# Linear stages of a two-block transformer: the three products of each row tile in a row, in place of three passes

## The chip, the cores and the metric

One core of a Trainium2 chip runs the whole program. The metric is device time in microseconds (us), as the median of several executions. Engines: PE is TensorE's matmul row and PEld its weight loads, DVE is VectorE, ACT is ScalarE, POOL is GpSimd, SP is SyncE, which issues the DMAs.

## The reference, cut to what matters

Two different transformer blocks of two layers each work on 512 tokens of width 1024, in float32. In each layer a norm is followed by a wide projection, several attention or convolution branches, gates, an output projection, another norm and a feed-forward pair. What matters here are the projections:

```
h = rms_norm(x, g_mix)
z = h @ w_in                       # 1024 x 7000 or so, cut into raw, misc, glu, gate parts
x = x + (g_a * o_a + g_b * o_b + g_c * o_c) @ w_out
h = rms_norm(x, g_ffn)
x = x + jnp.square(jax.nn.relu(h @ w_ff1)) @ w_ff2
```

The second block has the same shape, with its own mixers and a gated convolution in the feed-forward part (`h @ w_up`).

## The kernel before

Activations lie transposed: 128 features on the partitions, 512 tokens along the row, eight such tiles (k = 0 to 7) for a width of 1024. A **chunk** of weights is 128x1024 float32 (512 KB): eight tiles of 128x128, which together give 128 output features of 512 tokens. So a chunk is one PSUM bank of output, summed over the eight row tiles k.

The matrix engine gets operands rounded to a shorter float (fp32r), and precision is kept by splitting both operands in a high and a low part. ACT copies a chunk to `w_hi` (line 208, `weights_hi`), POOL subtracts that from the chunk and gives `w_lo` (line 214, `weights_lo`). For the activations ACT writes `a_hi` (line 226, or 240 with a bias) and DVE `a_lo` (line 231, or 253). The product is hi by hi plus hi by low plus low by hi: 24 matmuls of 128x128 by 128x512 for a chunk, all into one bank (line 276, `split_products`).

Before the change these are three passes over k. Each pass takes one weight part and one activation part. The wait for `w_hi` stands ahead of the first pass, the wait for `w_lo` ahead of the pass that uses it: the third, or the second in a *fresh* chunk. A fresh chunk is the first of a stage, or of each turn of its loop, where the stage also splits its activations: the first pass then waits for each `a_hi` tile (`fresh[0]`, a semaphore that ACT raises) and the third for each `a_lo` tile (`fresh[1]`, raised by DVE).

Both `w_hi` and `w_lo` have two slots (chunk j uses slot j % 2). ACT may write chunk j's slot when chunk j-2 is through PE (`chunk_done`), and POOL follows ACT. The raw chunk lies in a ring of four; SP loads four chunks ahead when `lo_ready` says that POOL is through with one. In most stages ACT or DVE copies the bank out (`evac`), and ACT does that ahead of the next `w_hi`. PE waits for an evacuation counter ahead of each chunk; where ACT holds the counter of the stage's first chunk, that counter is raised only after ACT's eight activation splits (line 326).

Stages follow each other with a barrier of all engines between. These go through `split_products`, per layer, with their chunks:

- block one: raw 12 (fresh), misc1 2, glu 8, gate 24, wout 8 (fresh, evacuated by DVE), ff_up 32 (fresh)
- block two: raw 8 (fresh), misc2 2 (the second chunk is multiplied first), fox 8, gate 16, wout 8 (fresh, by DVE), gated_up 44 (fresh)

That is 344 chunks over both layers. The down, merge and token-major products (lines 427, 954, 1122) have loops of their own and keep their passes.

Of the kernel before, what the change touches and what calls it, by code (L numbers as in the profile page):

```python
# [33 lines left out]
KD = D // P  # L34
# [224 lines left out]
def unit_tile(w, u):  # L259
    return w[:, u * P:(u + 1) * P]  # L260


def split_products(pe, m, base, i, j, body, bank, hi_ready, lo_ready, fresh=None):

    w_hi, w_lo = m.w_hi[:, j % 2, :], m.w_lo[:, j % 2, :]
    hi_hi, hi_lo, lo_hi = (w_hi, m.a_hi, hi_ready), (w_hi, m.a_lo, None), (w_lo, m.a_hi, lo_ready)
    order = (hi_hi, lo_hi, hi_lo) if fresh else (hi_hi, hi_lo, lo_hi)
    for p, (w, a, ready) in enumerate(order):  # L270
        if ready:
            pe.wait_ge(ready, i * body + j + 1)
        for k in range(KD):
            if fresh and p != 1:
                pe.wait_ge(fresh[p // 2], k + 1)
            mm = m.nc.tensor.matmul(bank, unit_tile(w, k), a[:, k, :], start=(p == 0 and k == 0), stop=(p == 2 and k == KD - 1))  # L276
    return mm


def linear_stage(m, base, iters, body, evac, source=None, make=None, post=None, extra="", dve_side=None,  # L280
# [10 lines left out]
    with stage(m, "chunk_done hi_ready lo_ready made src_hi src_lo act_evac dve_evac " + extra) as (block, (  # L291
# [15 lines left out]
        @block.tensor  # L307
        def _(pe):
            pe.sem_inc(chunk_done, 1)
            with loop(pe, iters) as i:  # L310
                for g in range(body):
                    who = evac[g][0]

                    pe.wait_ge(counters[who], i * len(mine[who]) + mine[who].index(g) + 1)
                    split_products(pe, m, base, i, g, body, m.ps[:, g, :], hi_ready, lo_ready,
                                   (src_hi, src_lo) if source and g == 0 else None).then_inc(chunk_done, 1)
            if pe_last:
                pe_last(pe, *side)
# [808 lines left out]
def misc1_stage(m):  # L1127
# [4 lines left out]
    with stage(m, "chunk_done hi_ready lo_ready rows_out gates_turned v_done gates_sig") as (block, (  # L1132
# [9 lines left out]
        @block.tensor  # L1142
        def _(pe):
            pe.sem_inc(chunk_done, 1)
            split_products(pe, m, base, 0, 0, 4, m.ps[:, 0, :], hi_ready, lo_ready).then_inc(chunk_done, 1)

            split_products(pe, m, base, 0, 1, 4, m.ps[:, 1, :], hi_ready, lo_ready).then_inc(chunk_done, 1)
            pe.wait_ge(lo_ready, 4)
            for t in range(TT):
                for half in range(2):  # L1150
                    mm = token_major(m, m.ps[:, 3 + t, 0:256], t, half, range(4 * half, 4 * half + 4), 256,
                                     lambda w, k: w[:, (k % 4) * 256:(k % 4 + 1) * 256], half == 0, half == 1)
                mm.then_inc(v_done, 1)
                if t == 0:
                    pe.wait_ge(rows_out, 1)
                    for t_ in range(TT):
                        tr = nc.tensor.transpose(m.ps[:, 2, t_ * 24:(t_ + 1) * 24], rows[:, t_ * P:(t_ + 1) * P], m.ident[0:24, 0:24])
                    tr.then_inc(gates_turned, 1)
# [1209 lines left out]
```

## Time and profile before

| | us |
|---|---|
| runs of the kernel | 4314.12, 4320.37, 4319.99; median 4319.99 |
| span of the profiled execution, first to last instruction | 4316.0 |
| PE busy in it | 3854.6 (89%) |
| POOL busy | 1494.6 (35%) |
| ACT busy | 1326.4 (31%) |
| DVE busy | 2193.7 (51%) |

No time of its own is given for the profiled execution beside its span. The three runs lie between 1.9 us below and 4.4 us above that span, the median 4.0 us above, so what lies around the span is a few microseconds. In the timeline a row is a merged group of like instructions: start, length of the group, engine, line, operation, out<-in, count, and the idle time before it with what ended it. PE and PEld are one engine: a weight load overlaps the matmul before it.

### The profile page before, as it was taken

The page shows a single profiled execution, that of the slowest core. Times are in us where ns is not written, and L with a number is a line of the kernel's source. Part 1 is how long each engine was busy: PE and PEld are TensorE (multiplying, and loading weights), DVE is VectorE, ACT ScalarE, POOL GpSimd, SP SyncE. Part 2 cuts the span into 40 slices and gives each one's busy share as a digit, 9 for nine tenths or more (in the row PEclk, how much of TensorE's full clock was granted, in tenths as well). Part 3 has the DMA queues.
Part 4 walks back from the last instruction along what each step waited for, and adds up shares of the span by engine and source line. Part 5 has one row for each costly group of instructions (what it writes and reads, how often), then busy time and mean ns, then how long its engine had stood idle before and what let it go on. Part 6 is the DMA issues. An engine that isn't in the chain of part 4 may idle for free. (4 is left out here: it accounts for less than half of the span.)

```text
span 4316.0 us, 48327 instructions
## 1 busy us (share of the span) xinstructions
PE 3854.6 (89%) x16004; PEld 2873.4 (67%) x16012; DVE 2193.7 (51%) x3287; ACT 1326.4 (31%) x2232; POOL 1494.6 (35%) x642
## 2 busy tenths in 40 slices
PE   6969999899979699999999779998999779999997
PEld 5614587687867145777778655686878654777876
DVE  1184568612221746586222356644883275546863
ACT  2212323322222133232322223433332233423332
POOL 3150044344431500443444342143544350334542
PEclk9857999999988679999999889999999888999998
DMA  3200022233422000222224211252324110622233
GB/s 113 78 0 1 7 91 88 74 97 107 146 82 79 12 1 1 83 88 83 85 100 145 85 50 39 98 173 76 97 89 170 61 59 1 212 90 82 94 131 122
DMA packets 99583, 354.77 MB, mean 82 GB/s; under 512 B 11888, under 2 KB 12528, under 8 KB 99312
## 3 DMA queue, kind: packets, MB, share of 16 engines
q1 hardware_dynamic: 99440, 352.96, 24.5%
q8 instruction: 78, 1.28, 0.1%
q14 instruction: 65, 0.53, 0.0%
HBM read 350.75 MB, written 2.10 MB: 82 GB/s over the span
## 5 line engine op out<-in xcount | busy, mean ns | idle before, releaser
L214 POOL TENSOR_TENSOR weights_lo<-arena,weights_hi 128x1024 fp32r<-128x1024 f32 x504 | 1301.8, 2585 | 2384.9 <-ACT weights_hi L208 2384.9
L276 PE MATMUL ps<-moving_hi,weights_hi 128*128 128x512 f32 x2752 | 717.0, 404 | 106.6 <-ACT weights_hi L208 40.5
L208 ACT ACTIVATE weights_hi<-arena 128x1024 fp32r<-128x1024 f32 x524 | 550.9, 1054 | 775.1 <-PE ps L427 403.0
L276 PE MATMUL ps<-moving_lo,weights_hi 128*128 128x512 f32 x2752 | 688.7, 392 | 2.6 <-DVE moving_lo L231 1.7
L276 PEld LDWEIGHTS ps<-moving_hi,weights_hi 128*128 128x128 f32 x2752 | 534.2, 195 | 231.7 <-issue 65.7
L276 PE MATMUL ps<-moving_hi,weights_lo 128*128 128x512 f32 x2752 | 683.0, 390 | 0.0
L276 PEld LDWEIGHTS ps<-moving_lo,weights_hi 128*128 128x128 f32 x2752 | 522.2, 190 | 116.2 <-DVE moving_lo L231 6.7
L276 PEld LDWEIGHTS ps<-moving_hi,weights_lo 128*128 128x128 f32 x2752 | 520.1, 189 | 109.0
L1574 DVE SCALAR_TENSOR_TENSOR arena<-arena 128x1024 f32<-128x1024 f32 x128 | 191.6, 1509 | 416.5 <-DMA arena<-modw_first 344.7
L776 PE MATMUL ps<-arena 64*128 64x512 f32 (+11 forms) x640 | 278.7, 536 | 41.8 <-PEq L120 38.7
L1438 DVE SCALAR_TENSOR_TENSOR arena<-arena 128x512 f32<-128x512 f32 x240 | 257.8, 1151 | 0.0
L427 PE MATMUL ps<-moving_hi,weights_hi 128*128 128x512 f32 x864 | 219.3, 397 | 25.8 <-ACT moving_hi L226 25.8
L881 ACT ACTIVATE arena<-ps,arena 128x512 f32<-128x512 f32 (+1 forms) x320 | 165.8, 524 | 203.2 <-DVE arena L827 202.4
L427 PE MATMUL ps<-moving_lo,weights_hi 128*128 128x512 f32 x864 | 217.1, 394 | 4.7 <-DVE moving_lo L231 4.7
L427 PE MATMUL ps<-moving_hi,weights_lo 128*128 128x512 f32 x864 | 213.4, 389 | 0.0
L427 PEld LDWEIGHTS ps<-moving_hi,weights_hi 128*128 128x128 f32 x864 | 165.4, 192 | 61.8 <-issue 27.3
L827 DVE TENSOR_REDUCE arena<-ps 128x1 f32<-128x512 f32 (+1 forms) x320 | 146.3, 488 | 112.3 <-PE ps L777 100.6
L800 PE MATMUL ps<-arena 128*64 128x512 f32 (+3 forms) x640 | 191.9, 443 | 9.8 <-DVE arena L855 9.8
L231 DVE TENSOR_TENSOR moving_lo<-arena,moving_hi 128x512 fp32r<-128x512 f32 x212 | 177.3, 889 | 43.9 <-ACT moving_hi L226 43.9
L1501 DVE TENSOR_TENSOR arena<-arena x64 | 44.3, 693 | 302.2 <-ACT arena L1499 302.2
L427 PEld LDWEIGHTS ps<-moving_lo,weights_hi 128*128 128x128 f32 x864 | 164.0, 190 | 41.5 <-DVE moving_lo L231 7.4
L427 PEld LDWEIGHTS ps<-moving_hi,weights_lo 128*128 128x128 f32 x864 | 162.4, 188 | 33.9
(253 smaller groups left out, 4183.0 us busy)
## 6 DMA issues: line engine op xcount, KB each, us to landing
arena<-wstream SPq DMA_DIRECT2D x532, 512.0 KB, 3.3
arena<-modw_first SPq DMA_DIRECT2D x64, 512.0 KB, 4.1
arena<-modw SPq DMA_DIRECT2D x64, 512.0 KB, 5.3
arena<-xT SPq DMA_DIRECT2D x1, 2048.0 KB, 10.4
outT<-arena SPq DMA_DIRECT2D x1, 2048.0 KB, 7.4
arena<-con SPq DMA_DIRECT2D x1, 1431.5 KB, 11.1
arena<-par SPq DMA_DIRECT2D x4, 136.0 KB, 3.2
arena<-arena SPq DMA_DIRECT2D x32, 2.0 KB, 1.7
```

The lines of the kernel that those rows point to most:

```text
L208: m.nc.scalar.activation(m.w_hi[:, j % 2, :], slab(m, base + j), ACT.Copy).then_inc(hi_ready, 1)
L214: m.nc.gpsimd.tensor_tensor(m.w_lo[:, j % 2, :], slab(m, base + j), m.w_hi[:, j % 2, :].bitcast(F32), ALU.subtract)\
L231: return m.nc.vector.tensor_tensor(m.a_lo[:, k, :], tile, m.a_hi[:, k, :].bitcast(F32), ALU.subtract)
L276: mm = m.nc.tensor.matmul(bank, unit_tile(w, k), a[:, k, :], start=(p == 0 and k == 0), stop=(p == 2 and k == KD - 1))
L427: mm = nc.tensor.matmul(m.ps[:, 4 * half + n, :], unit_tile(w[:, j % 2, :], 2 * n + k), a[:, 2 * h + k, :], start=(first and p == 0 and k ...
L776: nc.tensor.matmul(o, queries(j)[:, qt * P:(qt + 1) * P], keys(j, b)[:, 0:w], start=True, stop=False)
L800: mm = nc.tensor.matmul(m.ps[64 * half:64 * half + 64, 6 + j // 2 % 2, kt * P:T], values(j, b)[:, kt, :], pt[:, PT_AT[kt]:PT_AT[kt] + T - ...
L827: r = nc.vector.tensor_reduce(mx[:, 4 * (u % 2) + qt:4 * (u % 2) + qt + 1], m.ps[:, bank, c:c + P * (qt + 1)], AX, ALU.max, negate=True)
L881: a = nc.scalar.activation(prob[:, u % 2, qt, 0:P * (qt + 1)], m.ps[:, bank, c:c + P * (qt + 1)], ACT.Exp, bias=mx[:, s:s + 1], accum_out= ...
L1438: nc.vector.scalar_tensor_tensor(m.conv[:, c, :], up[:, c, bass.ds(i, T)], w[:, c, bass.ds(i, 1)], m.conv[:, c, :], ALU.mult, ALU.add).the ...
L1501: post=lambda dve, n: nc.vector.tensor_tensor(m.hidden[:, n, :], m.hidden[:, n, :], m.hidden[:, n, :], ALU.mult))
L1574: m.nc.vector.scalar_tensor_tensor(acc, weights, column(m.con("cvec", KD), k), acc, ALU.mult, ALU.add).then_inc(mod_added, 1)
```

## The change

The loop over passes becomes a loop over k, with the three products of tile k behind each other. Both weight parts are waited for ahead of the first matmul of a chunk, and a fresh chunk waits for `a_hi` and `a_lo` of tile k ahead of tile k's three matmuls. The number of matmuls, of weight loads and of DMAs stays, and so does every buffer.

```
-    for p, (w, a, ready) in enumerate(order):
-        if ready:
-            pe.wait_ge(ready, i * body + j + 1)
-        for k in range(KD):
-            if fresh and p != 1:
-                pe.wait_ge(fresh[p // 2], k + 1)
-            mm = m.nc.tensor.matmul(bank, unit_tile(w, k), a[:, k, :], start=(p == 0 and k == 0), stop=(p == 2 and k == KD - 1))
+    pe.wait_ge(hi_ready, i * body + j + 1)
+    pe.wait_ge(lo_ready, i * body + j + 1)
+    for k in range(KD):
+        if fresh:
+            pe.wait_ge(fresh[0], k + 1)
+            pe.wait_ge(fresh[1], k + 1)
+        m.nc.tensor.matmul(bank, unit_tile(w_hi, k), m.a_hi[:, k, :], start=(k == 0), stop=False)
+        m.nc.tensor.matmul(bank, unit_tile(w_hi, k), m.a_lo[:, k, :], start=False, stop=False)
+        mm = m.nc.tensor.matmul(bank, unit_tile(w_lo, k), m.a_hi[:, k, :], start=False, stop=(k == KD - 1))
```

## Rows read from the trace of the kernel before

**Rows 1.** The page: span, and busy time of each engine.

```profile
span 4316.0 us, 48327 instructions
...
PE 3854.6 (89%) x16004; PEld 2873.4 (67%) x16012; DVE 2193.7 (51%) x3287; ACT 1326.4 (31%) x2232; POOL 1494.6 (35%) x642
```

**Rows 2.** Groups of instructions: count, busy us, mean ns, idle before.

```profile
L276 PE MATMUL ps<-moving_hi,weights_hi 128*128 128x512 f32 x2752 | 717.0, 404 | 106.6 <-ACT weights_hi L208 40.5 <-ACTq L326 23.7 <-ACT moving_hi L240 23.6
L276 PE MATMUL ps<-moving_lo,weights_hi 128*128 128x512 f32 x2752 | 688.7, 392 | 2.6 <-DVE moving_lo L231 1.7
```

**Rows 3.** Timeline: a steady chunk of block one's ff_up.

```profile
957.24 1.77 PEld L276 LDWEIGHTS ps<-moving_hi,weights_hi 128*128 128x128 f32 x8
...
959.06 1.77 PEld L276 LDWEIGHTS ps<-moving_lo,weights_hi 128*128 128x128 f32 x8
...
959.39 2.39 POOL L214 TENSOR_TENSOR weights_lo<-arena,weights_hi 128x1024 fp32r<-128x1024 f32 x1 [3.05 <-ACT weights_hi L208]
960.87 1.77 PEld L276 LDWEIGHTS ps<-moving_hi,weights_lo 128*128 128x128 f32 x8
...
962.68 0.41 PEld L276 LDWEIGHTS ps<-moving_hi,weights_hi 128*128 128x128 f32 x2
```

**Rows 4.** Timeline: start of the fox stage, first of block two.

```profile
2565.20 2.00 ACT L208 ACTIVATE weights_hi<-arena 128x1024 fp32r<-128x1024 f32 x2 [5.81 <-PEq L120]
...
2566.33 2.39 POOL L214 TENSOR_TENSOR weights_lo<-arena,weights_hi 128x1024 fp32r<-128x1024 f32 x1 [12.91 <-ACT weights_hi L208]
2566.37 1.35 PEld L276 LDWEIGHTS ps<-moving_hi,weights_hi 128*128 128x128 f32 x4 [8.45 <-issue]
```

**Rows 5.** Timeline: start of the misc2 stage, first layer.

```profile
2507.06 4.70 POOL L214 TENSOR_TENSOR weights_lo<-arena,weights_hi 128x1024 fp32r<-128x1024 f32 x2 [9.48 <-ACT weights_hi L208]
2507.98 3.06 PEld L276 LDWEIGHTS ps<-moving_hi,weights_hi 128*128 128x128 f32 x8 [3.58 <-ACT weights_hi L208]
```

**Rows 6.** Timeline: PE released by POOL's low part, behind the fox stage.

```profile
2615.47 2.36 POOL L214 TENSOR_TENSOR weights_lo<-arena,weights_hi 128x1024 fp32r<-128x1024 f32 x1 [8.93 <-ACT weights_hi L208]
...
2617.89 0.50 PEld L1122 LDWEIGHTS ps<-weights_hi,moving_hi 128*128 128x128 f32 x2 [5.55 <-POOL weights_lo L214]
```

**Rows 7.** Timeline: start of block one's raw stage.

```profile
35.59 4.90 DVE L231 TENSOR_TENSOR moving_lo<-arena,moving_hi 128x512 fp32r<-128x512 f32 x8
35.95 3.06 PEld L276 LDWEIGHTS ps<-moving_hi,weights_hi 128*128 128x128 f32 x8 [6.35 <-issue]
```

**Rows 8.** Timeline: start of block one's wout stage.

```profile
796.43 8.87 DVE L231 TENSOR_TENSOR moving_lo<-arena,moving_hi 128x512 fp32r<-128x512 f32 x8 [1.98 <-ACT moving_hi L226]
796.51 0.19 PEld L276 LDWEIGHTS ps<-moving_hi,weights_hi 128*128 128x128 f32 x1 [5.13 <-issue]
...
804.15 0.19 PEld L276 LDWEIGHTS ps<-moving_lo,weights_hi 128*128 128x128 f32 x1 [0.92 <-DVE moving_lo L231]
...
805.46 1.81 PEld L276 LDWEIGHTS ps<-moving_hi,weights_hi 128*128 128x128 f32 x8
```

**Rows 9.** Timeline: the third chunk of block two's gate stage.

```profile
2779.80 3.48 POOL L214 TENSOR_TENSOR weights_lo<-arena,weights_hi 128x1024 fp32r<-128x1024 f32 x1 [5.69 <-ACT weights_hi L208]
...
2781.81 1.77 PEld L276 LDWEIGHTS ps<-moving_hi,weights_hi 128*128 128x128 f32 x8
```

**Rows 10.** Timeline: gated_up, the sixth chunk and one from its middle.

```profile
3011.39 2.51 POOL L214 TENSOR_TENSOR weights_lo<-arena,weights_hi 128x1024 fp32r<-128x1024 f32 x1 [4.99 <-ACT weights_hi L208]
...
3012.83 1.77 PEld L276 LDWEIGHTS ps<-moving_hi,weights_hi 128*128 128x128 f32 x8
...
3107.88 2.76 POOL L214 TENSOR_TENSOR weights_lo<-arena,weights_hi 128x1024 fp32r<-128x1024 f32 x1 [3.18 <-ACT weights_hi L208]
...
3110.75 1.32 PEld L276 LDWEIGHTS ps<-moving_hi,weights_hi 128*128 128x128 f32 x6
```

**Rows 11.** Windows, each one chunk: length, busy, then PEclk third from the end.

```profile
105.36:110.71 5.35, 5.35 (x24) 4.43 (x24) 0.00 (x0) 0.90 (x1) 4.74 (x2) 1.00 0.32 99
580.80:587.76 6.96, 6.93 (x24) 5.56 (x25) 6.96 (x6) 0.83 (x1) 5.00 (x2) 0.75 0.35 99
```

## Prediction

> **What bounds the kernel now.** I read the page first. PE is busy 3854.6 of 4316.0 us, 89% [rows 1]; no other engine is over 51%. In the groups by line the three products of line 276 are each 2752 matmuls, 344 chunks of 24 in all, and the idle time ahead of them is small: 106.6 us ahead of the high by high product, 40.5 of it waiting for ACT's high part of the weights, and 2.6 ahead of high by low [rows 2]. None of it is a wait for POOL's low part. So the changed stages are bound by PE, and PE's idle time lies at their starts.
>
> A steady chunk in the timeline shows why. Its passes start their loads at 957.24, 959.06 and 960.87, and the next chunk's at 962.68 [rows 3]: 5.44 us for 24 matmuls, 226.7 ns each. POOL makes the next chunk's low part from 959.39 to 961.78 (start plus 2.39). So when the next chunk starts at 962.68, its low part is 0.90 us old, though the passes don't want it before their third pass (second in a fresh chunk), 3.6 or 1.8 us later. I call 0.90 the **slack**: the old order has 1.8 or 3.6 us more of it than the new one, which wants `w_lo` at the chunk's first product. The question of the change is where slack, so counted, is negative.
>
> **Matmuls themselves: 0.** The same matmuls and loads are issued. Each of the three successions that the new order repeats (high-high to high-low, high-low to low-high, low-high to high-high) stands already at a boundary between passes or chunks, and there the loads keep their 227 ns: 1.81 or 1.82 us from each group's start to the next [rows 3]. The bank is one bank before and after. A fresh chunk gets eight waits more in the same place as the eight that are there, carried by the load or by a short instruction between two loads. The boundary between chunks has such instructions too, and its pace is unbroken. I take 0. The upper bound is some 0.05 us, the gap between the end of a load group (1.77) and the next group's start (1.82), for each of 8 waits in the fresh chunks (3+1+8 and 1+1+11 per layer, so 50 in two layers): 20 us. I don't put it in the sum, since in the rows that gap is there with and without such an instruction.
>
> **Starts of stages that aren't fresh.** In fox ACT's first high part releases PE at 2566.37, and POOL starts the low part at 2566.33, 2.39 long [rows 4]. Passes leave POOL until the third pass; the new order starts when POOL is through, at 2566.33+2.39 plus the time from POOL's end to a load. That time is 0.06 us (2615.47+2.36 = 2617.83 to 2617.89) [rows 6]. So PE starts 2.41 us later, and as everything behind it in the chain (next high part, evacuation, next chunk, the barrier) follows PE, the stage ends as much later. The timeline gives the same at glu and block two's gate (2.41), misc1 (2.47) and block one's gate (2.55, DVE's convolution slows POOL there). In the latter DVE ends 0.5 us ahead of PE, so it hides nothing. Misc2 multiplies its second chunk first: POOL must be through with both, 2507.06+4.70+0.06 = 2511.82, against a start at 2507.98: 3.84 [rows 5]. Twice each: 2 x (3 x 2.41 + 2.47 + 2.55 + 3.84) = **32.2 us**.
>
> **Fresh starts.** In raw PE already waits until ACT's eight splits are done: its first load is at 35.95. DVE's first `a_lo` is ready one eighth into its run of 4.90 us, at about 36.27; with 0.06, PE starts 0.39 later [rows 7]. Then DVE gives a tile every 0.61 us and three matmuls take 0.68 at full clock, so PE is behind DVE and its remaining work is unchanged. By the same reading ff_up pays 0.55, block two's raw and gated_up 0.62. Twice each: **4.4 us**. Wout is different, as DVE holds its evacuation and PE starts with the first `a_hi`, 796.51 [rows 8]. There the old third pass waits for the sixth `a_lo` (804.15) and ends 805.46. DVE brings the last three tiles 0.60 apart; the new order has nine matmuls of 0.227 left at 804.15 where the old had three: 804.15+2.04 = 806.19, **0.73** later, four times **2.9 us**. That holds if PE has got through its first 15 matmuls by 804.15, which it can from about 798.9 even with some of them slow.
>
> **Inside the stages.** The weights of chunk j follow the end of chunk j-2, so a shifted start shifts them along. I went through all chunks with the slack of each. Most have room: 0.9 and 1.5 in raw, 0.9 in ff_up, 0.3 to 0.6 in block one's gate, 0.4 in fox, 0.2 in wout, 0.11 (3107.88+2.76 = 3110.64 to 3110.75) and 0.6 by turns in gated_up. They are negative at these places. In gated_up the sixth chunk's low part is ready at 3013.90, 1.07 after 3012.83 [rows 10]: 1.10 us with latency, per layer. In block two's gate DVE adds weight rows beside POOL and ACT swaps tables: the third chunk is late by 2779.80+3.48-2781.81 = 1.47 [rows 9], others by 0.4 to 0.8. A stall lets the next chunk's parts catch up, so of two late neighbours the larger counts: 3.5 us in the first layer, 2.7 in the second. Wout's third chunk in block two adds 0.17 twice, raw's second 0.06. Sum 6.2 + 2.2 + 0.4 = **8.8 us**.
>
> **The clock.** After a pause PE may run at 1.2 GHz for a while. Misc1's first chunk came after 2.94 us of idle loads and took 5.35 us at clock 1.00; block one's gate after the same 2.94 took 6.96 at 0.75 [rows 11]. So 2.94 is a pause that may or may not cost 1.61 us. With 5.4 us of pause I expect misc1 to pay: **3.2 us** in two layers. The other starts pay already (chunks of 6.96 to 8.09), and longer pauses cost them nothing more, or move their slow stretch partly into the wait. The Trainium skill says in "TensorE: Matmul & The Clock Gate", section "HAM oscillation", that gaps between bursts of matmuls throw the array back to the half clock, and that one should avoid them; it speaks against this change. By it all twelve longer pauses could cost, by the trace only two of them have anything left to lose.
>
> **Sum.** 32.2 + 4.4 + 2.9 + 8.8 + 3.2 = 51.5 us. Against the profiled span 4316.0 that is 4367.5. The median of the runs lies 4.0 above that span, so the forecast is 4319.99 + 51.5 = about 4372, 1.2% slower. A measurement of this kernel tells apart about 0.2%, 8.6 us.
>
> **Rivals.**
>
> *Every pause costs clock.* If each of the twelve longer starts loses another 1.61 us instead of two, that is 19.3 in place of 3.2: 4388. For it: two equal pauses of 2.94 gave both outcomes. Against it: ten of the starts have their slow stretch already.
>
> *The slow stretch falls into the wait.* The opposite: a clock that is low for a fixed stretch after a pause is back when the matmuls start 2.4 us later. Ten starts gain up to 1.6 instead: 51.5 - 16 = 36: 4356. Against it: it rises again only with work.
>
> *Thin slack breaks.* Gated_up's 0.11 is 0.05 over the latency, and gate's stalls hang on when DVE and POOL meet. If 0.1 is missing in 42 chunks of gated_up (4 us) and each second chunk of gate pays 0.8 (12 in place of 6.2), 10 more: 4382.
>
> *The reload becomes free (faster).* The new order loads the same high tile twice in a row. If PE could skip or shorten the second load, the interval of 226.7 could fall to the streaming time of 512 columns at 2.4 GHz, 213.3: 13.3 ns on 2752 matmuls, 37 us, and twice that if the load behind it gets room as well, 73. Then 4319.99 + 51.5 - 73 = 4298. It decides from 51.5/2752 = 18.7 ns saved per triple. Against it: loads of 1.77 for eight [rows 3] already lie under the matmuls. The Trainium skill's same page says, in "What happens when you issue a matmul", that weights can be loaded once and used by many matmuls; it gives 215.7 ns for warm back-to-back matmuls of 512 columns, by which the first figure would be 30 us. But the program still issues each load.
>
> *The wait is hidden.* If other engines, not PE, ended these stages, nothing would move: 4320. Against it: PE's end is followed by the barrier in the windows that I read.
>
> **How the numbers follow.** Forecast (4372, own range 4362 to 4380) 0.52; all pauses 0.14; thin slack 0.16; slow stretch hidden 0.13; free reload 0.02; hidden wait 0.03. The range 4348 to 4396 takes in the middle four with their own spread, and the upper end the 20 us bound of the waits in part. Slower 0.95, within 0.2% 0.03, faster 0.02.
>
> **What would show it.** In fox, glu and gate the first load follows POOL's end by 0.06 instead of ACT's; misc2's waits for two low parts; a new wait of line 276 for POOL's `weights_lo` of about 45 us in the list of waits; wout's first chunk 0.7 longer; steady chunks still 5.44; misc1's first chunk near 7. Wrong would be: steady chunks of other length (reload, extra waits), or stalls in gated_up each second chunk.

## The result, and the profile after

The median of the kernel after is 4525.73 us (4525.10 to 4528.15, four runs) against 4319.82 us before: a recorded ratio of 1.0483, interval 1.0469 to 1.0498 (here and below the recorded ratios differ from the quotients of the medians by up to 0.0006). That is 205.9 us slower where 52 were forecast, far outside the range of 4348 to 4396. The sign was right and the size was not.

The page of the kernel after, span, busy times and groups, against [rows 1, 2]:

```profile
span 4526.4 us, 48753 instructions
...
PE 3877.2 (86%) x16004; PEld 2889.4 (64%) x16012; DVE 2092.3 (46%) x3287; ACT 1326.5 (29%) x2232; POOL 1603.0 (35%) x642
...
L214 POOL TENSOR_TENSOR weights_lo<-arena,weights_hi 128x1024 fp32r<-128x1024 f32 x504 | 1410.2, 2800 | 2478.1 <-ACT weights_hi L208 2478.1
L276 PE MATMUL ps<-moving_hi,weights_hi 128*128 128x512 f32 x2752 | 1099.2, 399 | 299.2 <-POOL weights_lo L214 217.9
L277 PE MATMUL ps<-moving_lo,weights_hi 128*128 128x512 f32 x2752 | 1091.4, 397 | 0.0
L278 PE MATMUL ps<-moving_hi,weights_lo 128*128 128x512 f32 x2752 | 1090.0, 396 | 0.0
```

PE's busy time grew by only 22.6 us, 3854.6 to 3877.2, while the span grew by 210.4. The difference is idle time, and the first product names what ends it: POOL's low part, 217.9 us. The prediction said "about 45". The list of PE's waits says how these are spread (total us, times, longest us):

```profile
PE ps L276 <- POOL weights_lo L214: 217.9, 24, 70.5
```

So 24 waits, and two of them are 70.5 and 70.4 us long. (The other 77 us aren't all new: such a row counts the whole idle time ahead of a start, 10.67 us in fox for instance, of which 2.4 are the change's. So the 45 that the prediction named for this row was too low even without the two stalls.) Ask next for POOL's subtraction by its line (shortest, median and longest in ns):

```profile
L214 POOL TENSOR_TENSOR weights_lo<-arena,weights_hi x504: 2338/2395/73983, 29.6 to 4486.4; 128x1024 fp32r<-128x1024 f32 x168
```

The median of the 504 subtractions is 2.395 us, as before (2.396). One is 73.98 us long; before, the longest was 5.78. A second like it (73.92) lies in the other layer. Both are the third subtraction of block one's gate stage. Around the first, the timeline of DVE, POOL, ACT and PE:

```profile
586.74 4.99 POOL L214 TENSOR_TENSOR weights_lo<-arena,weights_hi 128x1024 fp32r<-128x1024 f32 x2 [9.54 <-ACT weights_hi L208]
...
589.37 0.76 PE L276 MATMUL ps<-moving_hi,weights_hi 128*128 128x512 f32 x1 [4.92 <-POOL weights_lo L214]
589.43 35.99 DVE L1440 SCALAR_TENSOR_TENSOR arena<-arena 128x512 f32<-128x512 f32 x51
...
597.72 0.60 ACT L1492 ACTIVATE arena<-ps 128x512 f32 x1 [10.11 <-PE ps L278]
598.22 1.05 ACT L208 ACTIVATE weights_hi<-arena 128x1024 fp32r<-128x1024 f32 x1
...
599.35 73.98 POOL L214 TENSOR_TENSOR weights_lo<-arena,weights_hi 128x1024 fp32r<-128x1024 f32 x1 [7.61 <-ACT weights_hi L208]
...
654.50 16.64 DVE L1440 SCALAR_TENSOR_TENSOR arena<-arena 128x512 f32<-128x512 f32 x25
...
673.48 0.77 PE L276 MATMUL ps<-moving_hi,weights_hi 128*128 128x512 f32 x1 [70.46 <-POOL weights_lo L214]
```

In the kernel before, POOL's first three subtractions of the stage are these:

```profile
580.76 5.04 POOL L214 TENSOR_TENSOR weights_lo<-arena,weights_hi 128x1024 fp32r<-128x1024 f32 x2 [9.54 <-ACT weights_hi L208]
589.91 2.67 POOL L214 TENSOR_TENSOR weights_lo<-arena,weights_hi 128x1024 fp32r<-128x1024 f32 x1 [4.11 <-ACT weights_hi L208]
```

Line 1440 is the convolution's loop on DVE (1438 before). Its last operation ends at 654.50 + 16.64 = 671.14. POOL's ends at 599.35 + 73.98 = 673.33, 2.19 behind it, which is nearly the 2.39 that such a subtraction takes. That reads as POOL shut out until DVE had nothing left, and doing its work then; runs 4 and 8 put this reading to the test. PE's first load follows 0.12 later (its matmul 0.15). In windows (length; busy of PE, PEld, DVE, ACT, POOL; granted clock; then two columns on DMAs) the stage splits in chunk 0, the stall, and the rest:

```profile
589.34:597.20 7.86, 7.83 (x24) 6.22 (x25) 7.86 (x10) 0.00 (x0) 2.40 (x1) 0.66 0.39 133
597.20:673.45 76.25, 5.82 (x26) 4.50 (x25) 73.93 (x112) 3.09 (x4) 74.10 (x2) 0.57 0.00 0
673.45:794.47 121.02, 120.99 (x527) 100.11 (x528) 0.00 (x0) 32.48 (x42) 50.00 (x21) 0.99 0.30 95
```

In 76.25 us PE works 5.82, and DVE runs through its 112 operations undisturbed. In the rest DVE has nothing, so the two engines, which used to overlap, follow each other. The convolution as a group, in the kernel before and then in the kernel after (busy us, mean ns):

```profile
L1438 DVE SCALAR_TENSOR_TENSOR arena<-arena 128x512 f32<-128x512 f32 x120 | 128.9, 1151 | 0.0
```

```profile
L1440 DVE SCALAR_TENSOR_TENSOR arena<-arena 128x512 f32<-128x512 f32 x120 | 81.7, 754 | 0.0
```

Before, DVE's 120 operations took 128.9 us because POOL's subtractions kept breaking in: an operation that met one lasted 2.88 us instead of 0.74. After, nothing breaks in and DVE needs 81.7.

By stage, both layers together (us more than before; "lead-in" is what is added between the last load of the linear stage ahead in this list and the stage's first load, with whatever lies between, "within" what is added from there to its last load; the first raw stage's lead-in is counted from DVE's first split, which comes 1.8 us sooner in this profile):

| stage | forecast | lead-in | within |
|---|---|---|---|
| block one: raw | 0.8 | 0.6 | 0.5 |
| misc1 | 8.1 | 5.0 | 3.1 |
| glu | 4.8 | 7.2 | 1.9 |
| gate | 5.1 | 5.1 | **146.2** |
| wout | 1.5 | 4.7 | -3.2 |
| ff_up | 1.1 | 1.6 | 1.3 |
| block two: raw | 1.3 | 4.6 | 2.3 |
| misc2 | 7.7 | 7.7 | -1.1 |
| fox | 4.8 | 4.9 | 0.4 |
| gate | 11.0 | 7.8 | 4.2 |
| wout | 1.8 | 5.1 | -2.5 |
| gated_up | 3.4 | 1.3 | 1.8 |
| sum | 51.5 | 55.7 | 155.0 |

Without the two stalls of 70.46 and 70.40 the sum is 69.8. So of the 159 us by which the span missed the forecast, 141 are one event per layer, and 18 are to be found elsewhere.

### The profile page after: what moved, and what is told of

The parts are those of the page before. It is cut to its first block and busy times, and to the rows that moved or that the text cites. A ratio compares the mean times of both kernels' runs of the same rounds, so it can differ in the third digit from the quotient of the medians.

```text
span 4526.4 us, 48753 instructions
## 1 busy us (share of the span) xinstructions
PE 3877.2 (86%) x16004; PEld 2889.4 (64%) x16012; DVE 2092.3 (46%) x3287; ACT 1326.5 (29%) x2232; POOL 1603.0 (35%) x642
## 5 line engine op out<-in xcount | busy, mean ns | idle before, releaser
L214 POOL TENSOR_TENSOR weights_lo<-arena,weights_hi 128x1024 fp32r<-128x1024 f32 x504 | 1410.2, 2800 | 2478.1 <-ACT weights_hi L208 2478.1
L276 PE MATMUL ps<-moving_hi,weights_hi 128*128 128x512 f32 x2752 | 1099.2, 399 | 299.2 <-POOL weights_lo L214 217.9
L277 PE MATMUL ps<-moving_lo,weights_hi 128*128 128x512 f32 x2752 | 1091.4, 397 | 0.0
L278 PE MATMUL ps<-moving_hi,weights_lo 128*128 128x512 f32 x2752 | 1090.0, 396 | 0.0
L277 PEld LDWEIGHTS ps<-moving_lo,weights_hi 128*128 128x128 f32 x2752 | 530.9, 193 | 110.6
L278 PEld LDWEIGHTS ps<-moving_hi,weights_lo 128*128 128x128 f32 x2752 | 529.0, 192 | 113.3
L1576 DVE SCALAR_TENSOR_TENSOR arena<-arena 128x1024 f32<-128x1024 f32 x128 | 178.8, 1408 | 442.1 <-DMA arena<-modw_first 356.0
L429 PE MATMUL ps<-moving_hi,weights_hi 128*128 128x512 f32 x864 | 220.5, 399 | 25.8 <-ACT moving_hi L226 25.8
L429 PE MATMUL ps<-moving_lo,weights_hi 128*128 128x512 f32 x864 | 220.5, 399 | 3.6 <-DVE moving_lo L231 3.6
L429 PE MATMUL ps<-moving_hi,weights_lo 128*128 128x512 f32 x864 | 214.2, 390 | 0.0
L829 DVE TENSOR_REDUCE arena<-ps 128x1 f32<-128x512 f32 (+1 forms) x320 | 146.2, 487 | 115.3 <-PE ps L779 103.9
L429 PEld LDWEIGHTS ps<-moving_lo,weights_hi 128*128 128x128 f32 x864 | 166.1, 193 | 41.2 <-DVE moving_lo L231 6.5
L429 PEld LDWEIGHTS ps<-moving_hi,weights_lo 128*128 128x128 f32 x864 | 163.3, 189 | 34.3
L778 PEld LDWEIGHTS ps<-arena 64*128 64x128 f32 (+2 forms) x640 | 108.8, 212 | 95.7 <-issue 79.7
```

Source lines behind the costliest of these rows:

```text
L214: m.nc.gpsimd.tensor_tensor(m.w_lo[:, j % 2, :], slab(m, base + j), m.w_hi[:, j % 2, :].bitcast(F32), ALU.subtract)\
L276: m.nc.tensor.matmul(bank, unit_tile(w_hi, k), m.a_hi[:, k, :], start=(k == 0), stop=False)
L277: m.nc.tensor.matmul(bank, unit_tile(w_hi, k), m.a_lo[:, k, :], start=False, stop=False)
L278: mm = m.nc.tensor.matmul(bank, unit_tile(w_lo, k), m.a_hi[:, k, :], start=False, stop=(k == KD - 1))
L429: mm = nc.tensor.matmul(m.ps[:, 4 * half + n, :], unit_tile(w[:, j % 2, :], 2 * n + k), a[:, 2 * h + k, :], start=(first and p == 0 and k ...
L778: nc.tensor.matmul(o, queries(j)[:, qt * P:(qt + 1) * P], keys(j, b)[:, 0:w], start=True, stop=False)
```

## The experiments

Two theories stood after the result. **Shut out:** POOL asks for its operands while DVE runs one two-operand operation after the other, and whether it gets in hangs on when it asks, so the new order costs 70 us by asking at the wrong time. **Order:** the interleaved matmuls themselves, or their extra waits, hold something up in this stage.

### 1. The new order everywhere but in this stage

```
+    if m.passes:        # set around block one's gate alone
+        (the three passes of before)
+    else:
+        (the new order)
```

> New order everywhere except in block one's gate stage, which keeps its three passes. The whole excess over my sum lies in that stage in the trace of after: one stall of 70.5 us per layer, in which PE waits for one POOL subtraction of 73.98 us. Starvation theory (POOL's request loses the port to DVE's back to back convolution operations, and which way it falls depends on when the request comes): both stalls go, 4525.7 - 2 x (73.1 + 2.6) = about 4374. Rival (the new order costs something in every stage and the gate only shows it most): it stays above 4420.

Measured: 4372.74 us (4371.14 to 4376.02) against 4319.09, ratio 1.0125, interval 1.0108 to 1.0142. The gate stage is as before: its lead-in is unchanged and its length differs by 0.03 and 0.05 us. In the list of waits:

```profile
PE ps L285 <- POOL weights_lo L214: 67.3, 19, 10.4
```

So 153 us of the 206 come from having the new order in one stage of twelve, and the rest of the change costs 53.6.

### 2. The old order with the wait of the new

```
+    if m.early:         # set around block one's gate alone
+        pe.wait_ge(lo_ready, i * body + j + 1)
     for p, (w, a, ready) in enumerate(order):
```

> The kernel before, with one wait more in block one's gate stage alone: PE waits for POOL's low part ahead of each chunk's first pass, and the passes stay. Starvation theory: PE starts 2.55 us later, the third subtraction comes at another moment against DVE's operations, and if it loses, the stage is longer by about 70 us per layer: 4320 + 5 + up to 141 = about 4466; if that moment happens to be a good one, 4325. Rival (the order of the products is what does it): 4325. A result near 4466 rules the rival out, one near 4325 decides nothing by itself.

The wait stands ahead of each chunk of the stage. Measured: 4466.14 us, one run, against 4319.09. PE's waits:

```profile
PE ps L278 <- issue: 141.0, 2, 70.6
```

and POOL's third subtraction in the timeline, with the load that follows it:

```profile
591.74 74.16 POOL L214 TENSOR_TENSOR weights_lo<-arena,weights_hi 128x1024 fp32r<-128x1024 f32 x1 [7.43 <-ACT weights_hi L208]
...
665.97 1.35 PEld L278 LDWEIGHTS ps<-moving_hi,weights_hi 128*128 128x128 f32 x4 [70.98 <-issue]
```

The list names no releaser ("issue"), but POOL is through at 591.74 + 74.16 = 665.90 and PE's first load follows 0.07 later. The matmuls are in passes, and the stall is there: 70.6 and 70.4 us. So the interleaving isn't needed; the wait for POOL ahead of the first pass is enough. That the extra waits themselves hold something up isn't ruled out by this run. Runs 4 and 10 do that: with all the waits of the new order the stall is gone in run 4, and with none of them it is there in run 10.

### 3. The same kernel, POOL asking a little later

My first form of the shut-out theory was that the moment within one DVE operation decides, early in it or late. Two short instructions on POOL ahead of each subtraction (about 0.09 us each) shift it:

```
     pool.wait_ge(hi_ready, ...)
+    for _ in range(m.late):      # 2, block one's gate alone
+        hold(pool, m)            # a semaphore increment
     (the subtraction)
```

> The changed kernel, with two semaphore increments on POOL between its wait for the high part and each subtraction in block one's gate stage, which make its request some 0.13 us later. In the trace of after the two starved subtractions came 0.507 and 0.573 us behind the start of the DVE operation then running, in a rhythm of 0.6625; in before the ones that got through came at 0.006 to 0.373 and 0.576 to 0.654. Starvation theory: at 0.64 and 0.04 both get through: both stalls go, about 4380. Rival (POOL is starved whenever DVE's operations follow without a gap and POOL is not there first): the stalls stay, 4526.

Measured: 4525.38 us, one run; the third subtraction of the stage:

```profile
600.05 73.80 POOL L216 TENSOR_TENSOR weights_lo<-arena,weights_hi 128x1024 fp32r<-128x1024 f32 x1 [7.80 <-ACT weights_hi L208]
```

Here POOL asked 0.03 to 0.04 us after a DVE operation had begun and was shut out; in run 2 it asked 0.33 and 0.54 us after one, and was shut out too; before, it asked at moments from 0.01 to 0.65 and got in. The moment within an operation doesn't decide. That form of the theory fell.

### 4. A pause in DVE's stream

```
     with dve.Fori(1, TAPS) as i:
         (four operations)
+        dve.wait_ge(tapped, i * CCH + CCH)
```

> The changed kernel; at the end of each of the 30 turns of the convolution loop DVE also waits until its last operation of the turn is finished, so that it has a moment with nothing in flight. Starvation theory: POOL gets in at the end of a turn, at most 2.65 us after it asks; no subtraction over about 5.5 us; the stage is at most a few us longer than in before, 4380 to 4395. Rival (something else holds POOL, such as the priority of DVE for as long as its queue has work): the stalls stay, 4526 and more.

Measured: 4409.70 us (4406.47 to 4412.34) against 4319.09, ratio 1.0206, interval 1.0189 to 1.0223. POOL's and DVE's timelines:

```profile
599.95 2.44 POOL L214 TENSOR_TENSOR weights_lo<-arena,weights_hi 128x1024 fp32r<-128x1024 f32 x1 [7.64 <-ACT weights_hi L208]
...
595.42 2.74 DVE L1440 SCALAR_TENSOR_TENSOR arena<-arena 128x512 f32<-128x512 f32 x4 [0.58 <-DVE arena L1440]
598.73 4.88 DVE L1440 SCALAR_TENSOR_TENSOR arena<-arena 128x512 f32<-128x512 f32 x4 [0.56 <-DVE arena L1440]
```

POOL asks 7.64 us after its last turn, as late as in the kernel after (7.61), and is through in 2.44. So POOL's own idleness isn't the cause; DVE's unbroken stream is. The time is 15 us above the upper end of what was expected: the pauses of 0.56 to 0.58 us in each of 30 turns make DVE's loop the last to end in the stage, and PE's next load comes 15.7 us behind the stage's last where it came 1.8 behind it before. That is 14 us in each layer, so the cure takes back 28 of the 141 us.

### 5 to 7. The kernel before, POOL asking later throughout the stage

The edit is that of run 3 on the kernel before, with 7, 14 and 21 short instructions.

> The kernel before, with 7 semaphore increments on POOL between its wait and each subtraction in block one's gate stage (about 0.09 us each, so its request comes some 0.6 us, one DVE operation, later). My theory of the moment within one DVE operation is dead: requests starved at 0.03, 0.33, 0.51, 0.54 and 0.57 us behind its start, and got through at nearly all of these elsewhere. What now separates them is how many DVE operations had run without a break: 5 or 6 where POOL got in, 11 or 12 where it starved. Run theory (there is a number between 7 and 11 from which DVE keeps the port): with 6 or 7 POOL still gets in, 4320 to 4325. Rival (the longer idle time of POOL ahead of the request, 7.4 us and more against 2.4 to 4.1, is what matters): idle 4.7 here, also 4320. So this run is the anchor of the next two.

> The same with 14 increments: the first request comes behind 8 DVE operations, the later ones behind 6 or 7. Run theory: gets in if the number is above 8, 4320 to 4330; otherwise starved until DVE is through, and since the passes want the low part only in their third, PE waits some 65 us per layer: about 4450.

> The same with 21 increments: 9 operations first, 7 or 8 later. Run theory: 4320 to 4330 or about 4450 by where the number lies. If 9 get in here and 11 didn't elsewhere, the number is 10 or 11.

Measured, one run each: 4315.30, 4315.00 and 4484.31 us against 4315.53. The first two change nothing; for the third subtraction POOL asks in the sixth DVE operation since its last turn, as before, since a later turn moves DVE along, and not in the seventh or eighth as expected. In the third it is the stage's first subtraction that is shut out. First POOL and DVE with 14 short instructions:

```profile
579.44 5.33 POOL L216 TENSOR_TENSOR weights_lo<-arena,weights_hi 128x1024 fp32r<-128x1024 f32 x2 [10.65 <-ACT weights_hi L208]
...
577.14 1.92 DVE L1435 TENSOR_SCALAR arena<-arena 128x512 f32<-128x512 f32 x4 [0.32 <-PEq L120]
578.98 6.34 DVE L1440 SCALAR_TENSOR_TENSOR arena<-arena 128x512 f32<-128x512 f32 x3
```

and with 21:

```profile
585.07 80.78 POOL L216 TENSOR_TENSOR weights_lo<-arena,weights_hi 128x1024 fp32r<-128x1024 f32 x1 [11.20 <-ACT weights_hi L208]
...
581.15 0.75 DVE L1418 SCALAR_TENSOR_TENSOR arena<-ps,arena 128x512 f32<-128x512 f32 x1 [10.13 <-PE ps L278]
582.23 1.92 DVE L1435 TENSOR_SCALAR arena<-arena 128x512 f32<-128x512 f32 x4 [0.33 <-PEq L120]
584.06 16.66 DVE L1440 SCALAR_TENSOR_TENSOR arena<-arena 128x512 f32<-128x512 f32 x25
```

With 14, POOL asks during the first operation of DVE's loop and gets in; with 21, it asks during the second and doesn't. The old order, then, has the same trap, and a delay of under 2 us springs it.

### 8. One pause

```
-    with dve.Fori(1, TAPS) as i:
+    (turns 1 and 2 written out)
+    dve.wait_ge(lo_ready, 3)        # the stage's third subtraction
+    with dve.Fori(3, TAPS) as i:
```

> The changed kernel, with a single wait more: DVE runs the first two turns (8 operations) of the convolution, then waits until POOL is through with the third chunk's low part, then runs the other 28 turns as before. Run theory: one break at the right time is enough, as each later request comes about 5 operations behind the last; the stalls go and DVE's loop takes its 129 us again: 4372, up to 4380 if DVE now ends the stage. Rival (every single request needs its own break, as in the kernel that waits in each turn): POOL starves at the fourth chunk instead, 4510.

Measured: 4382.70 us (4378.65 to 4383.53) against 4315.53, ratio 1.0152, interval 1.0135 to 1.0169. DVE and POOL in the timeline:

```profile
600.29 2.39 POOL L214 TENSOR_TENSOR weights_lo<-arena,weights_hi 128x1024 fp32r<-128x1024 f32 x1 [7.67 <-ACT weights_hi L208]
605.73 3.00 POOL L214 TENSOR_TENSOR weights_lo<-arena,weights_hi 128x1024 fp32r<-128x1024 f32 x1 [3.05 <-ACT weights_hi L208]
...
590.31 7.50 DVE L1441 SCALAR_TENSOR_TENSOR arena<-arena 128x512 f32<-128x512 f32 x8
603.08 12.35 DVE L1447 SCALAR_TENSOR_TENSOR arena<-arena 128x512 f32<-128x512 f32 x12 [5.28 <-POOL weights_lo L214]
```

One pause of 5.28 us in DVE's stream, with the new order left in all stages, removes both stalls. The subtractions behind it ask 3.05 us after the last one and get in, without any pause. So in this stage only the first late request matters. The time lies 3 us above the 4380 that was the upper end. This is also the price of the change with the trap taken out: 67.2 us, 1.5%.

### 9 to 11. The kernel before, only the third subtraction of each turn late

The edit of run 3 again on the kernel before, with `range(m.late if j == 2 else 0)`, and 8, 15 and 22 instructions. The third subtraction is the one that the change makes late.

> The kernel before; only the subtraction of the third chunk of each turn of block one's gate loop gets 8 increments ahead of it, about 0.75 us. So the two subtractions at the stage's start keep their place (in the run with 21 increments it was the first of them that starved, behind 4 products by the first tap and 2 operations of the loop). Run theory, counted in operations since POOL last had the port: the third chunk's request comes in the 7th; POOL has got in in the 6th and starved in the 11th. 4316 to 4322 if the limit is above 7, about 4320 + 2 x 65 = 4450 if it is at 7.

> The same with 15 increments, 1.4 us: request in the 8th operation. 4316 to 4322 or about 4450. Rival (starving comes from POOL's idle time, at least 7.4 us in the starved cases): idle is 5.5 here, no starving in this and the last, nor in the next (6.2).

> The same with 22 increments, 2.1 us: request in the 9th operation. 4316 to 4322 or about 4450.

Measured, one run each: 4316.89, 4469.60 and 4467.39 us against 4320.22. POOL's timeline with 8:

```profile
589.48 2.70 POOL L216 TENSOR_TENSOR weights_lo<-arena,weights_hi 128x1024 fp32r<-128x1024 f32 x1 [4.74 <-ACT weights_hi L208]
```

and with 15:

```profile
592.65 76.27 POOL L216 TENSOR_TENSOR weights_lo<-arena,weights_hi 128x1024 fp32r<-128x1024 f32 x1 [5.32 <-issue]
```

and with 22:

```profile
594.17 75.75 POOL L216 TENSOR_TENSOR weights_lo<-arena,weights_hi 128x1024 fp32r<-128x1024 f32 x1 [5.84 <-issue]
```

A request 4.74 us after POOL's last turn gets in, one 5.32 us after it doesn't. One DVE operation (0.66 us from start to start) lies between them, and it costs some 150 us in two layers; the stalls stand in both. PE's matmuls are those of the kernel before.

### 12. Time or number of operations

4.74 and 5.32 us are also the seventh and the eighth DVE operation. Here each of DVE's operations does half the columns, twice as many of them:

```
-        nc.vector.scalar_tensor_tensor(m.conv[:, c, :], up[:, c, bass.ds(i, T)], ...
+        (two of T // 2 columns each)
```

> The kernel before, with each convolution operation (and the product by the first tap) cut in two of 256 columns, 240 in place of 120 in the loop. At 5.44 us between requests POOL's next one then comes behind about 8 short operations in place of 4 or 5, and the third chunk's behind about 10 or 11. Run theory by count of operations: if the limit lies at or below 10, POOL starves from the third chunk on, about 4430 or more; run theory by time without a break (4.1 us got in, 7.4 didn't): nothing starves, 4320 to 4345, since more operations make DVE's loop longer.

Measured: 4500.52 us, one run, against 4320.22. POOL's and DVE's timelines:

```profile
582.78 4.83 POOL L214 TENSOR_TENSOR weights_lo<-arena,weights_hi 128x1024 fp32r<-128x1024 f32 x2 [9.54 <-ACT weights_hi L208]
591.95 93.67 POOL L214 TENSOR_TENSOR weights_lo<-arena,weights_hi 128x1024 fp32r<-128x1024 f32 x1 [4.33 <-ACT weights_hi L208]
...
588.33 11.96 DVE L1441 SCALAR_TENSOR_TENSOR arena<-arena 128x256 f32<-128x256 f32 x30
```

POOL asks 4.33 us after its last turn, earlier than the 4.74 that got in, and is shut out, for the whole of DVE's loop. It is the 12th DVE operation since its last turn (one per 0.40 us here). In this one run, that speaks for a number of operations and against a time.

The requests that decide, by the number of the DVE operation in which POOL asks, counted from its last turn (first layer; the second agrees in each):

| kernel | us since POOL's last turn | DVE operation | subtraction, us |
|---|---|---|---|
| before | 4.11 | 6th | 2.67 |
| before, 8 on the third | 4.74 | 7th | 2.70 |
| before, 15 on the third | 5.32 | 8th | 76.27 |
| before, 22 on the third | 5.84 | 9th | 75.75 |
| passes, wait first | 7.43 | 11th | 74.16 |
| after | 7.61 | 11th | 73.98 |
| after, POOL later | 7.80 | 12th | 73.80 |
| halves | 4.33 | 12th | 93.67 |
| after, pauses in DVE | 7.64 | 2nd since a pause | 2.44 |
| before, 14 on each, the stage's first | 10.65 | 6th, 5th since a pause | 2.52 |
| before, 21 on each, the stage's first | 11.20 | 7th, 6th since a pause | 80.78 |

The last row doesn't fit the others: the seventh gets in above, and here it doesn't.

## Why the prediction was wrong

**The step that failed** is in "Starts of stages that aren't fresh": block one's gate at "2.55, DVE's convolution slows POOL there", with "0.3 to 0.6 in block one's gate" as slack in "Inside the stages". The 2.55 was right to 0.01: the stage's lead-in grew by 2.56 in both layers. In the sum nothing stood for this stage behind its start; the trace shows a stall of 70.46 us there in one layer and 70.40 in the other. What failed is that I took the duration of the later subtractions from the old trace (2.67 for the third), where they ask 4.11 us after the last one, and carried it over to a request that comes at another time. The chain of the third subtraction is short enough to write down, before and after: POOL's second ends 585.80 (580.76 + 5.04) and 591.73; chunk 0's loads take 6.96 us from 580.80 and 7.86 from 589.34; ACT's evacuation and high part follow the end of chunk 0; POOL asks at 589.91 and 599.35. The first two subtractions don't wait for PE, and PE now starts after the first. So the distance grows by the 2.5 us of wait plus the 0.9 by which chunk 0 is slower at the lower clock: 4.11 becomes 7.61. Run 2 shows that the wait does it with passes too: 7.43, with a chunk 0 of 7.73 us.

By the runs with a late third request, 1.2 us of this 3.5 are enough, and 0.6 are not. The prediction had the pieces: a stream of DVE operations, and POOL slowed by it. It named as rival "thin slack breaks", with "gate's stalls hang on when DVE and POOL meet", but only for block two's gate and at 0.8 us each. The mechanism was half seen, in the wrong stage, and its price was read from the subtractions of the old trace rather than bounded by the length of the stream beside them, some 80 us.

The Trainium skill says in "SBUF — State Buffer", section "SBUF: two separate sides", that DVE and GpSimd share a port pair under an exclusive lock, so that a DVE operation with two SBUF operands and a GpSimd operation shut each other out for a whole instruction, whichever starts first. For one pair of operations the traces agree: DVE's lasts 2.88 us when POOL's runs. By that rule POOL would wait 0.7 us at most, an estimate from the 0.74 us that one such operation takes here. The 74 us go beyond it, and the measurement decides.

**Step by step.**

"Matmuls themselves: 0" held. Steady chunks stay at 5.44 us with their loads 0.227 apart, now one by one through the three products. Nothing is seen of the 20 us bound on waits, nor of the free reload: the same high tile loaded twice in a row is no faster. Four matmuls in a row of a steady chunk of ff_up, in the timeline of the kernel after, against [rows 3]:

```profile
960.08 0.39 PE L278 MATMUL ps<-moving_hi,weights_lo 128*128 128x512 f32 x1
960.30 0.39 PE L276 MATMUL ps<-moving_hi,weights_hi 128*128 128x512 f32 x1
960.53 0.39 PE L277 MATMUL ps<-moving_lo,weights_hi 128*128 128x512 f32 x1
960.76 0.39 PE L278 MATMUL ps<-moving_hi,weights_lo 128*128 128x512 f32 x1
```

"Starts of stages that aren't fresh" held in size: misc1 2.48 (forecast 2.47), gate 2.56 (2.55), misc2 3.83 (3.84), fox 2.43 and 2.46 (2.41), glu 2.26 in the first layer (2.41). The load follows POOL's end by 0.12 us in each of these, and not by the 0.06 of [rows 6]; POOL's subtraction ahead of it is that much shorter in gate (2.48 us for 2.53). Misc2's start in the timeline against [rows 5]: POOL's second ends 2684.57 + 2.34 = 2686.91, the first load follows at 2687.03.

```profile
2684.57 2.34 POOL L214 TENSOR_TENSOR weights_lo<-arena,weights_hi 128x1024 fp32r<-128x1024 f32 x1
...
2687.03 0.29 PEld L276 LDWEIGHTS ps<-moving_hi,weights_hi 128*128 128x128 f32 x1 [7.41 <-issue]
```

"Fresh starts": wout's 0.73 held as a sum in block one, by other parts than I thought. PE starts 2.33 and 2.41 later, since it needs `a_lo` too, and is 1.6 shorter from there: 0.7 and 0.8. Block one's raw and ff_up together cost 4.1 where 1.9 were forecast.

"Inside the stages": gated_up's sixth chunk came as forecast, against [rows 10]. POOL's low part is there at 3202.59 + 2.49 = 3205.08, and the first load that follows had 1.20 us of idle time ahead of it:

```profile
3202.59 2.49 POOL L214 TENSOR_TENSOR weights_lo<-arena,weights_hi 128x1024 fp32r<-128x1024 f32 x1 [4.98 <-ACT weights_hi L208]
...
3205.20 0.19 PEld L276 LDWEIGHTS ps<-moving_hi,weights_hi 128*128 128x128 f32 x1 [1.20 <-ACT arena L1877]
```

Its slack of 0.11 held: no stall in each second chunk. Block two's gate became 2.1 us longer per layer within the stage where 3.5 and 2.7 were forecast, against [rows 9], as the subtraction of the third chunk now takes 2.40 instead of 3.48:

```profile
2967.04 2.40 POOL L214 TENSOR_TENSOR weights_lo<-arena,weights_hi 128x1024 fp32r<-128x1024 f32 x1 [8.09 <-ACT weights_hi L208]
...
2969.56 0.19 PEld L276 LDWEIGHTS ps<-moving_hi,weights_hi 128*128 128x128 f32 x1 [0.55 <-issue]
```

Here too a duration of the old trace didn't carry over, this time in the change's favour.

"The clock": misc1 pays as forecast, 5.35 to 6.88 us against [rows 11]; the window of that chunk after:

```profile
106.68:113.56 6.88, 6.85 (x23) 5.56 (x24) 0.00 (x0) 0.00 (x0) 2.21 (x1) 0.76 0.48 152
```

"The other starts pay already" held in part only. First chunks of glu and block one's gate go from 6.96 to 7.84 and 7.86, at a clock of 0.66 in the gate's instead of 0.75: 0.9 us each that I had at nothing. In fox and misc2 they go from 7.93 to 7.80 and from 8.09 to 6.94 us in the first layer, from 7.29 to 7.86 and from 6.89 to 6.97 in the second. This lies between my forecast and the rival in which every pause costs another 1.61. The Trainium skill's warning about gaps between bursts ("TensorE: Matmul & The Clock Gate", section "HAM oscillation") is borne out at this size, and isn't what decides the kernel.

With the trap out of the way (run 8) the traces differ by 63.0 us over the stages. Against the forecast glu has 4.4 more, raw of block two 3.8, ff_up 1.9, block one's gate 1.8, its raw 1.4, and block two's gate 5.1 less; the others agree within 1.5. In run 1 the sum is 55.8. The lead-ins of glu's second layer (2.5 to 2.7 us more than in the first) and of block two's stages vary from one kernel to the next, between -6.3 and +7.1 for block two's gate, and I haven't traced that into the attention work that lies there. Kernels that leave these stages as they were vary as much: in run 9 the lead-in of glu's second layer is 3.0 us shorter and that of block two's gate 4.6 longer in the first layer, in run 2 glu's are 2.4 shorter and 2.6 longer. So the differences at glu and at block two's gate can't be put down to the change. Beyond the forecast these are 9 us in run 1, 12 in run 8 and 18 in the kernel after; what of them is clock, what is other work and what is this variation stays open.

**What is shown and what is argued.** Shown: the 153 us are the new order's in one stage (run 1); the wait does it without the order of matmuls (2); a pause in DVE's stream removes it (4, 8); a delay of POOL's third request by 1.2 us brings it into the kernel before, one of 0.6 doesn't (9, 10); a shorter time with more operations is shut out (12). Not shown is why. That DVE's operations overlap, each 0.74 us long and starting 0.66 after the one before, may leave POOL no gap, but they did so before as well. A count of seven in, eight out fits the other kernels and not run 7: there POOL asks in the seventh operation since its last turn, the sixth after a pause of 0.33 us in DVE's stream, and is shut out, while one operation earlier (run 6) it got in. Four of these six have one operand, and POOL's last turn lies 11.2 us back. A rule that covers this too stays open.

## What to carry to other kernels

When an edit delays one engine's request, don't take the duration of the operation behind it from the old trace if another engine runs a long unbroken stream over the same memory: its upper bound is the rest of that stream. Read for each such operation how many of the other engine's it arrives behind, and ask what the edit does to that number, including the clock of the chunk ahead. A wait that belongs to the third pass is there for free; moving it to the chunk's first product costs the producer's full time at each start of a stage (2.4 to 3.8 us here), and if such an order is wanted all the same, one pause in the stream at the right place is worth 143 us of the 206 here.

## What the runs showed of the hardware

In these runs a GpSimd subtraction of 128x1024 elements with two operands takes 2.39 us alone and 2.4 to 3.0 us beside a stream of DVE operations with two operands (128x512, one per 0.66 us), if it asks no later than in the seventh of them since its last turn. If it asks in the eighth or later, it isn't served until the stream has ended: 73.8 to 76.3 us with 120 operations in the stream, 93.7 with 240 of half the columns. The stream itself is faster for it, 81.7 us instead of 128.9. A single pause in the stream was enough (run 8), and behind it GpSimd got in at each request, one per 5.44 us. One case doesn't fit the count: in run 7 a stage's first request, in the seventh operation, waited 80.8 us.
